# Gate/up and down products of one weight half with both halves of the operand, as one matmul of 512 columns

## The reference, cut to what matters

```python
    h2 = rmsnorm(h_res, norm2_w[l])
    gu = h2 @ w_gate_up[l]
    h_res = h_res + (jax.nn.silu(gu[..., :D_FF]) * gu[..., D_FF:]) @ w_down[l]
out = rmsnorm(h_res, final_norm_w)
```

## Time and profile before

| what | value |
|---|---|
| median of 3 runs | 1271.36 us (1269.83 to 1273.02) |
| the profiled execution, its own time | 1272.51 us |
| its span, first to last instruction | 1270.0 us |
| PE busy | 1204.4 us, 95% of the span |
| DVE busy | 855.0 us, 67% |
| ACT busy | 633.5 us, 50% |
| POOL busy | 219.1 us, 17% |

### The profile page before, as it was taken

How to read it: one execution, slowest core, us unless ns; L and a number is a source line. 1 busy time by engine, 2 the same in 40 slices (tenths; PEclk the granted TensorE clock), 3 DMA queues, 4 the chain that set the end, 5 groups by cost and what they waited for, 6 DMA issues and landing times.

```text
span 1270.0 us, 26129 instructions
## 1 busy us (share of the span) xinstructions
PE 1204.4 (95%) x10864; PEld 1167.3 (92%) x10864; DVE 855.0 (67%) x1348; ACT 633.5 (50%) x1015; POOL 219.1 (17%) x243
## 2 busy tenths in 40 slices
PE   5998999999999999999999879999999999999997
PEld 5898998999999989999889779999999999999996
DVE  4753856757867666667689677786875777855554
ACT  6643545453655445545758743333234736544443
POOL 3100042002100150011100213462540051000000
PEclk9999999999999999999999889999999999999999
DMA  7555554445655654454636332323324665566663
GB/s 252 175 165 158 164 184 137 146 137 161 189 191 156 185 157 134 133 166 148 205 127 182 109 100 84 118 72 85 109 72 149 203 198 170 191 187 183 183 200 117
DMA packets 59909, 196.30 MB, mean 155 GB/s; under 512 B 6382, under 2 KB 14088, under 8 KB 59664
## 3 DMA queue, kind: packets, MB, share of 16 engines
q1 hardware_dynamic: 49248, 179.33, 45.7%
q10 hardware_dynamic: 10016, 12.90, 3.0%
q0 software_dynamic: 528, 2.40, 0.8%
HBM read 190.37 MB, written 4.23 MB: 153 GB/s over the span
## 4 chain that ended last, share of the span: by engine, by line
PE 84%; DVE 5%; ACT 4%; issue 3%; DVEq 2%; POOLq 1%; DMA 0%; ACTq 0%
PE stream_ps L306 18%; PE stream_ps L307 18%; PE stream_ps L321 14%; PE stream_ps L300 4%; PE stream_ps L301 3%; PE stream_ps L302 3%; PE stream_ps L2011 2%; PE free_ps L2230 2%; PE free_ps L2242 2%; PE stream_ps L2323 2%; DVE w_lo L292 2%; ACT w_hi L286 1%; PE stream_ps L357 1%; PE stream_ps L362 1%; PE stream_ps L358 1%
## 5 line engine op out<-in xcount | busy, mean ns | idle before, releaser
L292 DVE TENSOR_TENSOR w_lo<-raw,w_hi 128x1024 fp32r<-128x1024 f32 x342 | 429.1, 1264 | 200.8 <-ACT w_hi L286 199.1
L286 ACT ACTIVATE w_hi<-raw 128x1024 fp32r<-128x1024 f32 x342 | 356.3, 1052 | 58.8 <-PE stream_ps L2011 26.7
L306 PE MATMUL stream_ps<-h_hi,w_hi 128*128 128x256 f32 (+1 forms) x1376 | 344.0, 288 | 6.7 <-DVE h_lo L1331 3.1
L307 PE MATMUL stream_ps<-h_lo,w_hi 128*128 128x256 f32 (+1 forms) x1376 | 337.4, 282 | 0.0
L306 PEld LDWEIGHTS stream_ps<-h_hi,w_hi 128*128 128x128 f32 x1376 | 260.8, 190 | 12.8 <-issue 6.6
L307 PEld LDWEIGHTS stream_ps<-h_lo,w_hi 128*128 128x128 f32 x1376 | 261.1, 190 | 0.5
L321 PE MATMUL stream_ps<-h_hi,w_lo 128*128 128x256 f32 (+1 forms) x1328 | 185.6, 282 | 3.8 <-DVE w_lo L292 3.8
L321 PEld LDWEIGHTS stream_ps<-h_hi,w_lo 128*128 128x128 f32 x1328 | 170.1, 189 | 4.4 <-DVE w_lo L292 4.4
L300 PE MATMUL stream_ps<-h_hi,w_hi 128*128 128x256 f32 (+1 forms) x384 | 118.3, 308 | 9.6 <-DVE w_lo L292 4.3
L301 PE MATMUL stream_ps<-h_lo,w_hi 128*128 128x256 f32 (+1 forms) x384 | 110.6, 288 | 0.0
L302 PE MATMUL stream_ps<-h_hi,w_lo 128*128 128x256 f32 (+1 forms) x384 | 110.6, 288 | 0.0
(11 more groups left out here) (436 smaller groups left out, 2276.0 us busy)
## 6 DMA issues: line engine op xcount, KB each, us to landing
raw<-stream_dram SPq DMA_DIRECT2D x342, 512.0 KB, 3.8
gate_spill<-gate_out ACTq DMA_DIRECT2D x16, 128.0 KB, 2.4
decay<-gate_spill POOLq DMA_DIRECT2D x2, 640.0 KB, 10.7
xT<-xT_dram ACTq DMA_DIRECT2D x4, 272.0 KB, 7.9
wik<-wik_dram ACTq DMA_DIRECT2D x2, 544.0 KB, 5.7
mem_raw<-memT_dram ACTq DMA_DIRECT2D x2, 512.0 KB, 9.2
hankel<-rel_scratch POOLq DMA_DIRECT2D x1, 1024.0 KB, 8.9
x_spill<-xT ACTq DMA_DIRECT2D x1, 1024.0 KB, 7.7
```

Of the source, the lines that this page charges most:

```text
L286: nc.scalar.activation(w_hi[s][:, :, :], raw[:, s, :].rearrange("p (k n) -> p k n", k=KT), ACT.Copy).then_inc(hi_ready, 1)
L292: nc.vector.tensor_tensor(w_lo[s][:, :, :], raw[:, s, :].rearrange("p (k n) -> p k n", k=KT), w_hi[s][:, :, :].bitcast(F32), ALU.subtract) ...
L306: nc.tensor.matmul(ps, l_hi, r_hi, start=first, stop=False)
L307: nc.tensor.matmul(ps, l_hi, r_lo, start=False, stop=False)
```

## The change

`h_hi` and `h_lo`, and `f_hi` and `f_lo`, become the two planes of one tile each (`h_pair`, `f_pair`), so that one matmul can read both: the moving operand is then 2 x 256 columns, and the PSUM bank takes 512 numbers a partition, the sum with the high operand in its first half and the one with the low operand in its second. The low weight's 8 matmuls of 256 columns still go to the first half. The two halves have to be added: in gate and up by a `tensor_reduce` on DVE for each block (into `f_act` or `f_val`, after which Silu on ACT reads `f_act` in SBUF), in down by a second `tensor_tensor` add into `xT`. The first eight gate and up blocks, and all products elsewhere, stay as they were.

```diff
-        h_hi = sb("h_hi", [P, KT, T], F32R)
-        h_lo = sb("h_lo", [P, KT, T], F32R)
+        h_pair = sb("h_pair", [P, 2, KT, T], F32R)
+        h_hi, h_lo = (h_pair[:, i, :, :] for i in range(2))
...
-            f_hi = sb("f_hi", [P, FT, S], F32R, two)
-            f_lo = sb("f_lo", [P, FT, S], F32R, two)
+            f_pair = sb("f_pair", [P, 2, FT, S], F32R, two)
+            f_hi, f_lo = (f_pair[:, i, :, :] for i in range(2))
...
+        def sides(s):
+            return stream_ps[s][:, :].rearrange("p (i n) -> p i n", i=2)
...
+        def block_sides(pe, G, s, free, free_at, pair, nlo=None):
+            pe.wait_ge(hi_ready, 4 * G + s + 1)
+            pe.wait_ge(free, free_at)
+            if nlo:
+                pe.wait_ge(*nlo)
+            for k in range(KT):
+                if nlo and k == 4:
+                    pe.wait_ge(nlo[0], nlo[1] + 1)
+                nc.tensor.matmul(sides(s), w_hi[s][:, k, :], pair[:, :, k, :], start=k == 0, stop=False)
+            pe.wait_ge(lo_ready, 4 * G + s + 1 + SLOTS)
+            for k in range(KT):
+                mm = nc.tensor.matmul(stream_ps[s][:, 0:S], w_lo[s][:, k, :], pair[:, 0, k, :], start=False, stop=k == KT - 1)
+            mm.then_inc(blk_done, 1)
...
                     ahead(split_hi, act, G_GU + w, s)
                     if s % 2 == 0:
-                        act.wait_ge(blk_done, SLOTS + 4 * (G_GU + w) + s + 1)
-                        nc.scalar.activation(f_act[:, s // 2, :], stream_ps[s][:, 0:S], ACT.Silu).then_inc(fact_ready, 1)
+                        act.wait_ge(pre_ready, 2 * w + s // 2 + 1)
+                        nc.scalar.activation(f_act[:, s // 2, :], f_act[:, s // 2, :], ACT.Silu).then_inc(fact_ready, 1)
...
                     ahead(split_lo, dve, G_GU + w, s)
+                    if s % 2 == 0:
+                        dve.wait_ge(blk_done, SLOTS + 4 * (G_GU + w) + s + 1)
+                        nc.vector.tensor_reduce(f_act[:, s // 2, :], sides(s).rearrange("p i n -> p n i"), AX, ALU.add).then_inc(pre_ready, 1)
                     if s % 2 == 1:
                         f = bass.ds(2 * w + s // 2, 1)
                         dve.wait_ge(blk_done, SLOTS + 4 * (G_GU + w) + s + 1)
+                        nc.vector.tensor_reduce(f_val[:, s // 2, :], sides(s).rearrange("p i n -> p n i"), AX, ALU.add)
+                        nc.vector.drain()
                         dve.wait_ge(fact_ready, 2 * w + s // 2 + 1)
-                        nc.vector.tensor_tensor(f_val[:, s // 2, :], stream_ps[s][:, 0:S], f_act[:, s // 2, :], ALU.mult).then_inc(dve_evac, 2)
+                        nc.vector.tensor_tensor(f_val[:, s // 2, :], f_val[:, s // 2, :], f_act[:, s // 2, :], ALU.mult).then_inc(dve_evac, 2)
...
-                        nc.vector.tensor_tensor(xt, stream_ps[n // 3][:, 0:S], xt, ALU.add).then_inc(dve_evac, 1)
+                        nc.vector.tensor_tensor(xt, stream_ps[n // 3][:, 0:S], xt, ALU.add)
+                        nc.vector.drain()
+                        nc.vector.tensor_tensor(xt, stream_ps[n // 3][:, S:2 * S], xt, ALU.add).then_inc(dve_evac, 1)
...
                     else:
-                        block_cols(pe, G_GU + w, s, dve_evac, D2 + 40 + 4 * w + s + 1, hS_hi, hS_lo,
-                                   (nlo_ready, 2 * LAYERS + 3) if (w, s) == (EARLY, 0) else None)
+                        block_sides(pe, G_GU + w, s, dve_evac, D2 + 40 + 4 * w + s + 1, h_pair[:, :, :, tok],
+                                    (nlo_ready, 2 * LAYERS + 3) if (w, s) == (EARLY, 0) else None)
...
-                        with_hi(stream_ps[c][:, 0:S], w_hi[s][:, k, :], f_hi[:, kf, :], f_lo[:, kf, :], kf == 0)
+                        nc.tensor.matmul(sides(c), w_hi[s][:, k, :], f_pair[:, :, kf, :], start=kf == 0, stop=False)
```

## The result

The changed kernel takes 1300.05 us, the median of six runs (1292.86 to 1301.19), against 1272.17 us before (six runs, 1266.8 to 1274.33): **ratio 1.021, 95% interval 1.018 to 1.024**, or 28 us slower. 1297.9 us were forecast, in a range of 1289 to 1310.

What follows compares the result with a forecast made beforehand. PE bounds the kernel before; after the change a DVE and ACT ring bounds gate and up. 27.6 + 2.1 - 3.7 + 0.5 = +26.5 us on the profiled 1272.51 us gives 1299.0, corrected to a median of 1297.9 us, range 1289 to 1310.

Steps and rivals of the forecast that it cites:

- The ring: Gate and up: DVE and ACT hand-offs from one `f_val` product to the next take 7.03 us a pair, over PE's 5.68.
- The reduction: Gate and up: each DVE `tensor_reduce` from PSUM takes 0.68 us, with 0.42 and 1.22 us as bounds.
- Gate and up: Stage before down: its pairs at 7.03 us make down begin 27.6 us later.
- PE in gate and up: PE waits for `w_hi` twice a pair, pauses about 1.1 and 0.6 us, and is busy for 76%.
- The pause: Before down: PE has nothing to do for 7.7 us.
- The clock: Behind the pause before down: PE runs at half clock for a while, +2.1 us (bounds 1.7 and 2.4).
- Down: Down stage: 176 input tiles with a wide step of 0.216 instead of 0.237 us save 3.7 us.
- The second add: End of down: only the last output tile's extra add into `xT` is on the path to the norm, +0.5 us.
- A slow or short reduction: Two rivals, gate and up: reduction of 1.22 us gives 1317.3 us, chance 0.10; of 0.42 us gives 1288.5 us, chance 0.07.
- PE as the bound: Rival, gate and up: PE stays the bound and the kernel gets faster, 1262.2 us; chance 0.03.
- The clock did not fall inside gate and up: Denies a rival: half clock in gate and up for six of 18 pairs, +22 us, 1320 us; chance 0.04.
- wide products bring nothing: Rival: 512 columns cost two old steps, down saves nothing, 1301.6 us; inside the range, no chance of its own.

Runs made afterwards that it cites:

- e3: Changed kernel, but Silu reads PSUM directly and the gate's reduction works on unrelated SBUF numbers into a spare tile; 1267.42 us in one run.
- e4: Changed kernel with the gate's reduction issued twice, the first time into a spare tile nobody reads; 1306.60 us in one run.
- e5: Changed kernel reordered: on ACT both splits before Silu, `f_hi` and `f_lo` behind the next pair's first split; 1266.38 us, ratio 0.999 to before.
- e9: Changed kernel with only Silu moved on ACT, behind the pair's second split instead of between the two; ratio 1.001 to before.
- e8: Changed kernel with 30 unused products of constants on PE in the pause before down; 1298.57 us in one run.
- e1: Kernel before with 512-column products in down only, gate and up left as before; 1267.48 us, ratio 0.999.
- e12: Kernel before with only the normed operand's two halves laid side by side in one SBUF tile; 1264.62 us, ratio 0.997.
- e10: e5 with the two halves of `h_pair` and of `f_pair` side by side in SBUF; ratio 0.996 to before.
- e13: The kernel of e10 measured once more; 1262.31 us, ratio 0.996 to before.

## Why the prediction was right, point by point

- **The ring**, the step that decided. Forecast 7.03 us a pair, measured 7.09 us. Eight of the nine steps are within 0.01 us of the forecast (0.46, 0.32, 1.08, 1.14, 0.72, 0.32, 1.08, 1.14). The ninth, the last reduction to the product, took 0.83 us instead of 0.77 us: the drain, on which DVE waits for its own result, costs 0.15 us behind it and not 0.09 us. e3, e4, e5 and e9 show that it is a ring, by a cut, a longer step and a moved Silu.
- **The reduction**, the price that was unknown: 0.684 us for all of them, with 2 numbers a sum and 256 sums (forecast 0.68 us, bounds 0.42 and 1.22 us):

```profile
L1827 DVE TENSOR_REDUCE f_act<-stream_ps 128x256 f32<-128x512 f32 x17 | 11.6, 684 | 0.0
```

- **Gate and up.** Forecast +27.6 us, measured 127.82 - 98.45 = +29.4 us. 1.1 us is the drain, 18 times 0.06; 0.7 us are two products that came 0.35 us late, at 1093.67 and 1207.44 us, each marked `[0.49 <-issue]`. What stopped DVE there is open.
- **PE in gate and up** waits for `w_hi` and for nothing else, as forecast, but it is busy for 85% and not 76%, and its pauses are 0.5 us on average and 0.8 us at most, where 1.1 and 0.6 us were forecast. The forecast counted steps; a record lasts beyond the next start (eight narrow products 1.10 us, their steps 0.94 us), and the wide step is longer. The time does not hang on it.
- **The pause** before down: forecast 7.7 us, measured 7.71 us. **The clock** behind it: forecast 2.1 us, 1.5 us by e8.
- **Down**: the term that was mis-sized. A wide step took 0.229 us and not 0.216 us, so 176 of them save 1.4 us (e1) and not 3.7 us. The step of the float32 products was no guide to that of the fp32r ones. The Trainium skill, "TensorE: Matmul & The Clock Gate", section "Back-to-back issue gap", has the formula columns / 2.4 GHz + 2.5 ns, the same 216 ns for 512 columns; it gives it for an isolated matmul, and about 131 ns for 512 columns in a sustained stream. Neither is seen here, where the steps are 229 to 237 ns. The estimate that the prediction made from the formula, 3 ns gained on an input tile, errs less than its own of 21 ns: down gains 8 ns.
- **The second add** of the last output tile: forecast +0.5 us, measured nothing; the tail has 12.36 us before and 12.37 us now. The prediction had the last add on the path to the norm, but it is hidden there: PE has begun with the 16 sum-of-squares instructions, of which 14 don't need that tile. They take 3.0 us (14 x 0.216), until 1281.2 us, and the square is done at 1279.7 us:

```profile
1278.15 3.62 PE L417 MATMUL free_ps<-wide,cst 128*128 128x256 f32 x16
1278.35 0.42 DVE L1844 TENSOR_TENSOR xT<-stream_ps,xT 128x256 f32<-128x256 f32 x1 [1.73 <-PE stream_ps L2349]
1278.85 0.42 DVE L1846 TENSOR_TENSOR xT<-stream_ps,xT 128x256 f32<-128x256 f32 x1
1279.31 0.42 ACT L1126 ACTIVATE wide<-xT 128x256 f32<-128x256 f32 x1 [4.32 <-DVE xT L1846]
1281.81 0.47 ACT L408 ACTIVATE rstd<-free_ps,eps_col 128x256 f32<-128x256 f32 x1 [0.78 <-PE free_ps L417]
```

- **The sum** was 27.6 + 2.1 - 3.7 + 0.5 = 26.5 us; the measured terms are 29.4 + 1.5 - 1.4 + 0 = 29.5 us, and the medians differ by 27.9 us. The errors of the terms are +1.8, -0.6, +2.3 and -0.5 us, +3.0 us in all, so two of them took a little off the other two. That the forecast of 26.5 us is 1.4 us from the medians and not 3 us is luck with the noise: the interval of the ratio runs from 23 to 31 us and holds both sums.
- **The rivals.** A slow or short reduction and PE as the bound are excluded by the rows above. The clock did not fall inside gate and up: it was 1.00 from 1088 to 1211 us. That wide products bring nothing is half true: 8 ns of 237 in down, 3 ns or none in gate and up.

## What to carry to other kernels

An engine that is idle for 40% of a stretch may have no room for another instruction if it is one of two that hand work to and fro in written orders: add up the ring, step by step from start to start, before adding to it, and look for the one wait that closes it. Here it was a Silu between two splits, and moving it one place took the ratio from 1.021 to 1.001. Stages, and not spans, are to be compared where one execution loses 8.5 us more to half clock than another in code that nobody touched.

## What the runs showed of the hardware that was not expected

- Where the two halves of an operand lie in SBUF changes the step of narrow products that read only one of them, on average by 0.6 ns of 119: side by side 118.6 ns (e12), as two tiles 119.2 ns (before), for the low weight. Over some 5500 products of this operand the shorter steps come to about 3 us, an estimate from these traces; e12's median is 4.0 us (0.3%) under before. It is not the same everywhere: where the low weight's eight products stand in a row, their step of 256 columns falls from 118.1 to 117.1 ns, and where the three products of an input tile follow each other, the low weight's rises from 117.0 to 118.6 ns. What causes it is open.
- The wide step depends on the operand: 0.229 us for `f_pair`, 0.234 us for `h_pair` with far halves, 0.237 us with near ones, the last being no less than two narrow ones. The distance of the halves is not the cause in down; what is stays open too.
- Behind one and the same pause of 2.26 us, one execution of a kernel began down at half clock (e10) and another did not (e13).
- The share of half clock in unchanged code varies from run to run: the six runs of the changed kernel had mean clocks of 0.982 to 0.989, and the time goes with it (1301.19 us at 0.982, 1292.86 us at 0.989).
